# A two-block transformer kernel: first block's weave, gate product by parts, embedding weights applied in the routing

## The reference, cut to what matters

```python
def first_block(x, ...):
    h = rms_norm(x, norm_mix_pre); q, k, v, u, gates = split(h @ w_in)
    y_a = chunk_band_attention(q, k, v, rel_bias) @ w_attn_out
    y_b = multiscale_pool(u, w_pool_group, pool_scale) @ w_pool_out
    g_a, g_b = split(sigmoid(gates + b_gate))
    x = x + rms_norm((g_a * y_a + g_b * y_b) @ w_o, norm_mix_post)
    return x + rms_norm(conv_gated_ffn(rms_norm(x, norm_ffn_pre), ...), norm_ffn_post)

def second_block(x, p, ...):
    h = x + concat([diff_attention(...), neighbourhood_attention(...)]) @ w_out
    h = h + hier_moe(rms_norm_2(h, g_ffn), w_rg, w_re, w1, w3, w2)   # 32 experts, top 2
    return h + rms_norm_2(p @ w_ple, g_ple) * sigmoid(rms_norm_2(h, g_plg) @ w_plg)
```

## Time and profile before

| | us |
|---|---|
| median of 3 runs (1638.41 to 1641.41) | 1639.23 |
| the profiled execution | 1641.76 |
| its span, first to last instruction | 1639.7 |
| TensorE busy in it | 1569.1 (96%) |
| mean granted TensorE clock | 0.985 |

### The profile page before, as it was taken

One profiled execution on the slowest core, in us unless ns is written; L12 is line 12 of the kernel. 1 busy time (PEld: TensorE's weight loads), 2 busy tenths in 40 slices (PEclk: granted clock), 3 DMA queues, 4 the chain that ended last, 5 costly groups with the idle time before them and its releaser, 6 DMA issues. The chain is left out here.

```text
span 1639.7 us, 20000 instructions
## 1 busy us (share of the span) xinstructions
PE 1569.1 (96%) x7970; PEld 1105.5 (67%) x7970; DVE 724.5 (44%) x1228; ACT 532.8 (32%) x910; POOL 161.8 (10%) x170
## 2 busy tenths in 40 slices
PE   6999899999999999999999899999999999999969
PEld 5776588789888888887777777744444444444459
DVE  5334422445544444468565777521122222212364
ACT  5233422334433323344454667321100110110052
POOL 1012200101201111111300210010000000000000
PEclk9999999999999999999999989999999999999979
DMA  6111232222322222222110222749999999999921
GB/s 264 54 50 59 106 113 103 92 76 96 123 80 75 107 100 103 103 90 86 44 52 27 103 103 78 295 184 386 421 420 420 421 418 421 421 417 421 415 93 53
DMA packets 46158, 307.05 MB, mean 187 GB/s; under 512 B 5216, under 2 KB 7520, under 8 KB 10992
## 3 DMA queue, kind: packets, MB, share of 16 engines
q1 hardware_dynamic: 43344, 296.22, 45.6%
q0 software_dynamic: 2720, 9.52, 1.6%
HBM read 301.52 MB, written 4.19 MB: 186 GB/s over the span
## 5 line engine op out<-in xcount | busy, mean ns | idle before, releaser
L590 DVE TENSOR_TENSOR w_lo<-M,w_hi 128x2048 fp32r<-128x2048 f32 x73 | 169.2, 2323 | 192.8 <-ACT w_hi L585 192.8
L2379 PE MATMUL bank<-M 128*64 128x512 f32 x1024 | 229.1, 599 | 3.8 <-DMA M<-in_w 3.7
L585 ACT ACTIVATE w_hi<-M 128x2048 fp32r<-128x2048 f32 x73 | 139.0, 1910 | 163.6 <-PE bank L762 62.3
L762 PE MATMUL bank<-HTH,w_hi 128*128 128x512 f32 x432 | 168.1, 389 | 0.0
L762 PE MATMUL bank<-HTL,w_hi 128*128 128x512 f32 x432 | 168.1, 389 | 0.0
L762 PE MATMUL bank<-HTH,w_lo 128*128 128x512 f32 x432 | 168.0, 389 | 0.0
L2379 PEld LDWEIGHTS bank<-M 128*64 128x64 f32 x1024 | 71.6, 137 | 140.8 <-issue 139.8
L2396 PE MATMUL bank<-M 128*64 128x512 f32 x512 | 114.0, 596 | 1.9 <-DMA M<-in_w 1.9
L2510 DVE TENSOR_TENSOR X<-bank,X 128x512 f32<-128x512 f32 x72 | 48.1, 688 | 115.8 <-PE bank L2412 115.7
L762 PEld LDWEIGHTS bank<-HTL,w_hi 128*128 128x128 f32 x432 | 81.1, 188 | 16.9
L762 PEld LDWEIGHTS bank<-HTH,w_hi 128*128 128x128 f32 x432 | 81.1, 188 | 16.8
(11 more groups left out here) (338 smaller groups left out, 3014.7 us busy)
## 6 DMA issues: line engine op xcount, KB each, us to landing
M<-in_w SPq DMA_DIRECT2D x192, 1024.0 KB, 10.1
M<-in_wd SPq DMA_DIRECT2D x78, 1024.0 KB, 4.8
M<-in_nb SPq DMA_DIRECT2D x4, 1536.0 KB, 6.5
M<-in_rows POOLq DMA_DIRECT2D x5, 512.0 KB, 4.1
X<-in_x SPq DMA_DIRECT2D x4, 512.0 KB, 9.0
M<-in_tb POOLq DMA_DIRECT2D x8, 256.0 KB, 4.0
ple_raw<-M POOLq DMA_DIRECT2D x4, 512.0 KB, 2.9
M<-ple_raw SPq DMA_DIRECT2D x4, 512.0 KB, 6.9
```

The costliest lines, as they stand in the source:

```text
L585: e.activation(hi[:, :], slots[slot_of[n]], ACT.Copy).then_inc(split_hi_done, 1)
L590: e.tensor_tensor(lo[:, :], slots[slot_of[n]], hi[:, :], ALU.subtract).then_inc(split_lo_done, 1)
L762: m = e.matmul(out[:, :], w[:, k0 + k, n0:n0 + 128], v[k], start=(k == 0 and i == 0), stop=(k == len(hi) - 1 and i == 2))
L2379: m = e.matmul(b[64 * s:64 * s + 64, :], Xe[:, 4 * kh + k, o + C * s:o + C * s + C], unit_w(key, 4)[:, k, :], start=(kh == 0 and k == 0), ...
```

## The change

1. In the first attention "u 1" moves from steps 20, 21 to 16, 17, head pair 3's q and k from 16 to 19 to 18 to 21, and the split after unit "in 4" from step 21 to 18. Scores, turned weights, woven products, attention output and mix get banks of their own in place of turns of four. The first three quarters of y(0,0,0) and y(0,0,1) run at steps 33 and 34.
2. In the routing, ScalarE squares each half tile of the embedding product, and VectorE multiplies each tile by g_ple before it is stored. The row g_ple is then loaded where g_plg was; g_plg follows behind the fourth tile. XSH and XSL are stored to DRAM (2 MB each) from POOL's queue.
3. The last down product stands ahead of the last three pieces of scatter 7, and its second half makes one output half after the other. The table of the square root is loaded behind the last Silu.
4. The end moves into the first block of instructions, ahead of `overflow`. The gate's weights are laid out in units of 4 k-steps x 512 columns. For the first 512 columns, TensorE's order is the list END: n = transposes of a tile, a = high parts of both, b = low part of the tile with high part of the weights, c0 and c1 = high part of the tile with low part of unit 0 and 1. The second 512 columns follow tile by tile, the last tile in two halves of 256. Low parts of these weights are written in place into their slots. PN's root is applied in the last product.
5. `overflow` comes last. If its count isn't 0, it reads XSH and XSL back, runs its rounds, and computes the end once more (`again`).

```diff
-        PH, PL = ([overlay(f"{n}{i}", A0 + 14336 + o + 4096 * i, UNIT) for i in range(2)]
-                  for n, o in (("PH", 0), ("PL", UNIT)))
-        OS = overlay("OS", A0 + 20704, TT, C)
+        PH = [overlay(f"PH{i}", A0 + o, UNIT) for i, o in enumerate((0, 2048, 4096, 19456))]
+        PL = [overlay(f"PL{i}", UNIT * i, UNIT) for i in range(NS_MOE)]
+        OS = overlay("OS", A0 + 19968, TT, C)
...
-        for hp, at in ((1, (4, 5, 6, 7)), (2, (8, 9, 10, 12)), (3, (16, 17, 18, 19))):
+        for hp, at in ((1, (4, 5, 6, 7)), (2, (8, 9, 10, 12)), (3, (18, 19, 20, 21))):
...
-        for g, at in enumerate(((13, 14), (20, 21), (22, 23), (24, 25))):
+        for g, at in enumerate(((13, 14), (16, 17), (22, 23), (24, 25))):
...
+        Y_FIRST = {33: 0, 34: 1}
+        woven_turn = itertools.cycle((0, 1))
         for i in range(len(ATT) + 3):
             if i < len(ATT):
-                ps.put(("as", i), range(4))
+                ps.put(("as", i), [2 + i % 2])
             for key, j in A_WOVEN.get(i, ()):
                 if j == 0:
-                    ps.put(key, (4, 5))
+                    ps.put(key, [next(woven_turn)])
+            if i in Y_FIRST:
+                ps.put(("y", 0, 0, Y_FIRST[i]), [2 + Y_FIRST[i]])
             if 2 <= i <= len(ATT) + 1:
-                ps.put(("at", i - 2), range(4))
+                ps.put(("at", i - 2), [5 + 2 * (i % 2)])
             if i >= 3 and (i - 3) % 8 == 0:
-                ps.put(("ao", (i - 3) // 8), [6 + (i - 3) // 8 % 2], counted=False)
+                ps.put(("ao", (i - 3) // 8), [4 + 2 * ((i - 3) // 8 % 2)], counted=False)
             if i in MIX_AT:
-                ps.put(("mix", MIX_AT[i]), range(4))
-        for i in range(4):
-            for q in range(2):
-                for j in range(2):
-                    ps.put(("y", i, q, j))
-            for q in range(i == 0, 2):
-                for j in range(2):
-                    ps.put(("g", i, q, j))
+                ps.put(("mix", MIX_AT[i]), [4 if MIX_AT[i] == 3 else 5 + 2 * ((i - 1) % 2)])
+        for j in range(2):
+            ps.put(("y", 0, 1, j), [4 + j])
+        for j in range(2):
+            ps.put(("g", 0, 1, j), [6 + j])
+        by_turn = itertools.cycle(range(8))
+        for i in range(1, 4):
+            for v in ("y", "g"):
+                for q in range(2):
+                    for j in range(2):
+                        ps.put((v, i, q, j), [next(by_turn)])
...
-        MOE += scatter(6, 5, 6, 7) + scatter(7, *range(8)) + steps_of(NPAIR, 2) + scatter(8, *range(8))
+        MOE += scatter(6, 5, 6, 7) + scatter(7, *range(5)) + steps_of(NPAIR, 2) + scatter(7, *range(5, 8)) + scatter(8, *range(8))
...
+        END = [("n", 0), ("n", 1), ("a", 0), ("b", 0), ("n", 2), ("a", 1), ("b", 1), ("c0", 0), ("c0", 1), ("a", 2), ("c1", 0), ("c1", 1),
+               ("n", 3), ("b", 2), ("c0", 2), ("c1", 2), ("a", 3), ("b", 3), ("c0", 3), ("c1", 3)]
+        OUT = [(n, t, 0, 512) for n in range(2) for t in range(TT)][:-1] + [(1, 3, 0, 256), (1, 3, 256, 256)]
...
-        A_SPLIT = {4: ("in", 1), 6: ("in", 2), 8: ("in", 3), 21: ("in", 4), 22: ("in", 5), 24: ("in", 6), 27: ("in", 7)}
+        A_SPLIT = {4: ("in", 1), 6: ("in", 2), 8: ("in", 3), 18: ("in", 4), 22: ("in", 5), 24: ("in", 6), 27: ("in", 7)}
...
+                if i in Y_FIRST:
+                    for g in range(3):
+                        taken(e, ("ao", g))
+                    split_ready(e, ("ap", 0))
+                    y_pe(e, Y_FIRST[i], claim(e, ("y", 0, 0, Y_FIRST[i]))[0], range(3))
...
+        def y_pe(e, j, out, ks):
+
+            wh, wl = parts(("ap", 0), KD)
+            for k in ks:
+                for i, (w, v) in enumerate(((wh, ya[0][k]), (wh, ya[1][k]), (wl, ya[0][k]))):
+                    m = e.matmul(out[:, :], w[:, k, 128 * j:128 * j + 128], v, start=(k == i == 0), stop=(k == 3 and i == 2))
+            return m
 
...
-                        gemm3_T(e, ("ap", i), 128 * j, *claim(e, ("y", i, q, j)), *y, k0=4 * q)
+                        if i == q == 0:
+                            y_pe(e, j, bank[ps.at["y", 0, 0, j][0]], [3]).then_inc(fills_of(("y", 0, 0, j)), 1)
+                        else:
+                            gemm3_T(e, ("ap", i), 128 * j, *claim(e, ("y", i, q, j)), *y, k0=4 * q)
...
-            load_gain(e, 4)
+            o = BIG["ple"]
+            e.dma_start(rowb[:, :], rows_d[:, o:o + D].to_broadcast([128, D])).then_inc(d_rowb, 16)
+            for i, x in enumerate((XSH, XSL)):
+                e.dma_start(xs_d[i], x[:, :, :].bitcast(F32)).then_inc(d_xs, 16)
...
+            for k, h in [(0, 0), (1, 0), (0, 1), (1, 1)] if (p, kh) == (NPAIR - 1, 1) else [(0, 0), (0, 1), (1, 0), (1, 1)]:
...
+            at = TT * h + t
+            e.wait_ge(act_own.sem, act_own.n)
+            act_own.mark(e.activation(junk[:, 0, 0:512], b[:, :], ACT.Square, accum_out=PL_ST[0][:, at:at + 1]))
             e.activation(STAGE[t][:, h * 512:(h + 1) * 512], b[:, :], ACT.Copy).then_inc(empties, 1)
 
-        def ple_pool(e, t):
+        def ple_dve(e, t):
+
+            e.wait_ge(d_rowb, 48)
             for h in range(2):
                 taken(e, ("pl", t, h))
+            e.tensor_tensor(STAGE[t], STAGE[t], rowb[:, :], ALU.mult).then_inc(pl_row, 1)
+            if t == 3:
+                ss, sq, r = PL_ST
+                e.tensor_tensor(ss[:, 0:TT], ss[:, 0:TT], ss[:, TT:2 * TT], ALU.add).then_inc(pl_sum, 1)
+
+        def ple_pool(e, t):
+            e.wait_ge(pl_row, t + 1)
...
+                    if p == NPAIR - 1:
+                        act_own.mark(e.activation(one, one, ACT.Sqrt))
...
+                        for t in range(2):
+                            ple_dve(e, t)
+                if what == "pl" and at[1] == 1:
+                    ple_dve(e, at[0])
...
-            for t in range(2):
-                ple_pool(e, t)
...
+                    if g == 0:
+                        for t in range(2):
+                            ple_pool(e, t)
                 if what == "pl" and at[1] == 1:
                     ple_pool(e, at[0])
+                    if at[0] == 3:
+                        load_gain(e, 4)
...
+        TMP = [area(o, 512) for o in (21504, 22016, 28224)]
+
+        def gate_part(e, out, n, t, ks, x, low, start=False, stop=False, cs=slice(0, 512)):
+
+            for k in ks:
+                w = list(parts(("plg", 2 * n + k // 4), 4))[low]
+                m = e.matmul(out, x[:, k, t * 128:(t + 1) * 128], w[:, k % 4, cs], start=start and k == ks[0], stop=stop and k == ks[-1])
+            return m
+
+        def gate_hi(e, j):
+            e.wait_ge(split_hi_done, split_index(unit["plg", j]) + 1)
+
+        def end_pe(e):
+            first, second = range(4), range(4, 8)
+            for what, t in END:
+                if what == "n":
+                    norm_pe(e, 4, t)
+                    continue
+                out, fills = bank[ps.at["pg", 0, t, 0][0]], fills_of(("pg", 0, t, 0))
+                if what == "a":
+                    claim(e, ("pg", 0, t, 0))
+                    e.wait_ge(n_hi, 2 * (NORM_N[4] + t) + 2)
+                    for j, ks in enumerate((first, second)):
+                        gate_hi(e, j)
+                        gate_part(e, out[:, :], 0, t, ks, HTH, 0, start=(j == 0))
+                if what == "b":
+                    ht_ready(e, 4, t)
+                    gate_part(e, out[:, :], 0, t, range(KD), HTL, 0)
+                if what == "c0":
+                    split_ready(e, ("plg", 0))
+                    gate_part(e, out[:, :], 0, t, first, HTH, 1)
+                if what == "c1":
+                    split_ready(e, ("plg", 1))
+                    gate_part(e, out[:, :], 0, t, second, HTH, 1, stop=True).then_inc(fills, 1)
+            split_ready(e, ("plg", 3))
+            for n, t, o, w in OUT[TT:]:
+                b, fills = claim(e, ("pg", n, t, o))
+                cs = slice(o, o + w)
+                gate_part(e, b[:, 0:w], n, t, range(KD), HTH, 0, start=True, cs=cs)
+                gate_part(e, b[:, 0:w], n, t, range(KD), HTL, 0, cs=cs)
+                gate_part(e, b[:, 0:w], n, t, range(KD), HTH, 1, stop=True, cs=cs).then_inc(fills, 1)
+
+        def embed_root_act(e):
+
+            ss, sq, r = PL_ST
+            e.wait_ge(pl_sum, 1)
+            e.activation(sq, ss[:, 0:TT], ACT.Sqrt, scale=1.0 / D, bias=eps).then_inc(pl_sqrt, 1)
+
+        def end_act(e):
+            e.wait_ge(d_xs, 32)
+            for j in range(2):
+                split_act(e, unit["plg", j])
+            norm_act(e, 4, 0, 0)
+            norm_act(e, 4, 1, 0)
+            norm_act(e, 4, 0, 3)
+            norm_act(e, 4, 2, 0)
+            norm_act(e, 4, 1, 3)
+            norm_act(e, 4, 2, 3)
+            norm_act(e, 4, 3, 0)
+            split_act(e, unit["plg", 2])
+            embed_root_act(e)
+            norm_act(e, 4, 3, 3)
+            split_act(e, unit["plg", 3])
+            for i, (n, t, o, w) in enumerate(OUT):
```

(62 more changed lines are left out.)

249 lines of the change are left out of this document (126 added, 123 removed).

## The result

The change makes the kernel faster: 1618.89 us median of 4 runs (1618.06 to 1619.51), against 1638.82 for the kernel before beside it. The ratio is 0.9877, with a 95% interval from 0.986 to 0.9894. The profiled execution took 1619.18 us; I had 1618.7 for it.

What follows compares the result with a forecast made beforehand. TensorE, busy 96% of the span, was taken as the bound. Last product's end 1618.8 + 3.6 + 0.3 + 0.5 - 6.6 gave span 1616.6, 23.1 under 1639.7; from the median 1639.23 that is 1616.1, say 1616 us, range 1612 to 1622.

Steps and rivals of the forecast that it cites:

- First block: First attention block: moving the weight split gains 4.4 us and separate banks gain 2.2, together 6.6 (4 to 7).
- The stores of XS: Routing: the XSH and XSL stores, 2 MB each, fall into a hole in DMA traffic; cost 0, between 0 and 10 us.
- rival (a): Routing: the store of XS isn't hidden and pushes the full load stream, up to 10 us: 1618 to 1626; chance 0.10.
- The expert stage: Loading the second gain row at about 1102 us delays the full weight stream behind it: +0.5 us (0 to 1.2).
- The handover: End of expert stage: moved scatter pieces and the split last down product let scatter 8 start and end 2.2 us earlier.
- Tile 0's norm: Last norm's first tile: table load and between-block steps leave the path; TensorE turns tile 0 at 1568.4, not 1576.17.
- The product: Gate product at the end: 47.9 us of TensorE work without waits, plus 2.5 (0 to 5) for a clock fall.
- Behind it: After the last product: sigmoid, product, sum and store 3.6 us as before, plus 0.3 (0 to 1.5) for the branch.
- (d): Rival: XS rows leave SBUF slowly, the store blocks the stream beyond the hole, and the kernel is slower; chance 0.01.
- (b): Rival: the woven end stalls and the clock falls again, once or twice: 1620 to 1626; chance 0.15.
- (e): Rival: the first block's moves bring new waits or lose their gain, 2 us or less: 1620 to 1621; chance 0.07.
- (c): Rival: the clock never falls before tile 0 of the last norm: 1613.5; chance 0.25.

Runs made afterwards that it cites:

- undo_banks: Changed kernel with the pooled half of the first y product again claiming the banks of the two woven gate products; ratio 0.991 to the kernel before.
- undo_two: Changed kernel with 18 matmuls of the first y product back behind the last attention values and the last down product in its old order; ratio 0.9853 to the kernel before.
- xs_late: Changed kernel with the two stores of XSH and XSL issued later, by GpSimd behind its part of the third group's one-hot; ratio 0.992 to the kernel before.
- before_again: The kernel before, unchanged, run again for a second look at its expert stage; ratio 0.9999, span 1640.7 us.
- undo_split: Changed kernel with the fifth input unit's split back from step 18 to 21 and the woven projections in their old steps; ratio 0.9889 to the kernel before.
- two_ifs: Changed kernel with again() under a second branch of its own behind the first, with its own load of the count; ratio 0.9873 to the kernel before.

## Why the prediction was right or wrong

The sum came out 0.7 us short of the profiled span (1616.6 against 1617.3), because misses of both signs cancelled: 3.2 us too little behind the last product, 2.3 too much in the expert stage. That closeness is luck. In the order of its steps:

- **First block**, 6.6 predicted, 6.6 measured over the first block (262.44 and 255.87), 6.4 by the first up product. Both mechanisms were right, and the new wait of 0.4 us for YBL is in the 0 to 1 that I had set for the moved split. What failed is the way the sum was put: I added a gain of 4.4 and one of 2.2 as if each stood alone. undo_banks shows a wait of 6.0 us, and 8.9 in all, for the second once the first is made. The sum is right only since both were made.
- **The place of three quarters of y**: nothing predicted, nothing measured (undo_two).
- **The stores of XS**: 0 predicted, nothing seen in the stage, and xs_late shows what the hole was worth: the 10 us of rival (a), and the clock.
- **The expert stage**: +0.5 predicted for the gain row's load, -1.8 measured, 2.3 off. The step that failed is the term itself: I took the profiled execution's stage as the kernel's. Its wait of 2.9 us and the fall at 1523 come in some executions of either kernel, before_again's stage took 470.7, and after's was the shortest of ten. What the gain row's load costs is lost in this spread and stays open.
- **The handover**, 2.2 predicted, 1.36 measured. The moved pieces gave their 1.4. The step that failed is the reading of the earlier trace rows: "TensorE stood from about 1562.0, where ScalarE starts YH". ScalarE starts there because the first half of the row is done; the second half's product went on for another 0.73 us. In before too, then, only one high and one low part followed the product's end, 1.78 us in both kernels, and the new order had nothing to take.
- **Tile 0's norm**: scatter 8's start to the first transposes 6.05 predicted, 5.95 measured (1554.99 to 1560.94). The table load behind the last Silu is off the path, as said.
- **The product**: 50.4 predicted from the first transposes, 49.3 measured, without a gap. 47.9 of work stands. The clock's term was mis-sized: 2.5 against 1.06 (1.6 at most in the other executions). Its fall costs only what the chain can't hide, and VectorE's scale of tile 1 comes 1.5 us behind tile 0's (1559.60, 1561.06) whatever TensorE's clock.
- **Behind it**: 3.9 predicted, 7.1 measured, the largest miss, named beforehand as a sign of a wrong step. I priced the branch at 0.3 (0 to 1.5) as if it were the one of before moved to another place. It is not: its body got again() and so took the transposes and matmuls that TensorE jumps over from 104 to 200. In before TensorE's branch took 0.36 us. And it stands where nothing covers it.

Of the rivals none decided: (a) and (d) are refuted by the windows at 1056 to 1072, (b) by the chain without a gap, (e) by the marks. (c) didn't come in after; it came in two of the nine profiled executions, undo_two and undo_split, and is worth 1.06 to 1.6 us.

## What to carry to other kernels

When a branch skips a body, count the instructions of each engine in the body, TensorE's above all: a jump beyond what is fetched cost some 4 us here, where nothing covered it, and a hint 8 us ahead took all but 0.5 of it away. Two edits whose waits lie one behind the other on the same engine can't each be priced alone from the rows of before: made alone, the first only lengthens the second wait by what it gives. And where a stage is bound by transfers, one execution's waits are a sample; take a stage's length from several before you build on 1 or 2 us of it.

## What the runs showed beyond that

The price of a far jump: 3.99 (undo_banks) to 4.35 us (two_ifs) for TensorE's queue beyond the code at hand, in eight profiled executions, 0.40 within it, 0.50 with a hint 8 us ahead, 0.045 to 0.07 for the other engines.

How much of the scatter is the clock. 35 executions of the kernel before, on four chips, had spans from 1634.0 us (mean granted clock 0.994) to 1643.0 (0.983), with a correlation of -0.85 and 0.74 us for each 0.001. The same shows in single kernels: undo_two's four executions went from 1611.6 (0.997) to 1618.6 (0.991). Short waits of 1 to 3 us sometimes drop the clock and sometimes don't (2.07 us did in after, 2.06 didn't in undo_two), and where it could be measured ahead of tile 0, it cost 1.06 to 1.6 us. What decides it is not shown by these runs.
